# Output-projection products placed in the last head pair of a hybrid decoder step (one Trainium2 core)

## What is computed

```
h    = ada_norm(x)                                   # modulation from c @ w_ada
proj = h @ w_in
y_pool = pool_mixer(proj[:, :1024])                  # 8 tiles of 128 channels
y_rwkv = rwkv7(proj[:, 1024:])                       # 16 heads of 64 channels = 8 head pairs of 128
mix  = concat([y_pool, y_rwkv]) @ w_out              # 2048 x 2048
x    = x + gate * mix
h2   = ada_norm(x);  x = x + gate_m * moe(h2)        # 16 experts, top 2
```

## Time and profile before

| what | value |
|---|---|
| median of 3 runs | 2084.46 us |
| lowest and highest | 2076.31 and 2084.47 us |
| the profiled execution, own time | 2076.4 us |
| its span, first to last instruction | 2074.8 us |
| PE busy | 1912.3 us, 92% of the span |
| DVE, ACT, POOL busy | 593.2, 306.4, 453.4 us |
| mean granted TensorE clock | 0.968 |

### The profile page before, as it was taken

One profiled execution on the slowest core, in us unless ns is written; L12 is line 12 of the kernel. 1 busy time (PEld: TensorE's weight loads), 2 busy tenths in 40 slices (PEclk: granted clock), 3 DMA queues, 4 the chain that ended last, 5 costly groups with the idle time before them and its releaser, 6 DMA issues. The chain is left out here.

```text
span 2074.8 us, 27843 instructions
## 1 busy us (share of the span) xinstructions
PE 1912.3 (92%) x10685; PEld 979.8 (47%) x10685; DVE 593.2 (29%) x1326; ACT 306.4 (15%) x690; POOL 453.4 (22%) x585
## 2 busy tenths in 40 slices
PE   4579999999999986999699999999999999999996
PEld 2137665555555544776343344433444434444333
DVE  2152144445434543012312121222122222222213
ACT  2001122212221222001300011100011000111002
POOL 0020012112211221100003322233222332223333
PEclk9679999999999998999799999999999999999998
DMA  9894365546654652754089999999999999999992
GB/s 307 305 307 113 90 201 167 176 157 191 186 153 166 182 170 61 234 160 143 1 342 414 413 410 397 392 390 404 397 394 393 392 403 391 396 397 390 403 393 84
DMA packets 248447, 573.80 MB, mean 277 GB/s; under 512 B 10691, under 2 KB 114461, under 8 KB 230899
## 3 DMA queue, kind: packets, MB, share of 16 engines
q1 hardware_dynamic: 244574, 563.76, 73.8%
q0 software_dynamic: 3200, 6.20, 1.3%
q10 hardware_dynamic: 631, 3.27, 0.6%
HBM read 567.78 MB, written 5.65 MB: 276 GB/s over the span
## 5 line engine op out<-in xcount | busy, mean ns | idle before, releaser
L1761 PE MATMUL PS<-ring,xt 128*64 128x512 f32 x2048 | 523.9, 600 | 2.0 <-DVE xt L1873 1.4
L1963 POOL TENSOR_TENSOR x<-x,tmp 128x512 f32<-128x512 f32 (+1 forms) x192 | 244.7, 1276 | 721.6 <-DVE tmp L1882 721.6
L1882 DVE TENSOR_TENSOR tmp<-PS,catT 128x512 f32<-128x512 f32 (+1 forms) x192 | 132.2, 689 | 620.8 <-PE PS L1749 616.6
L1761 PEld LDWEIGHTS PS<-ring,xt 128*64 128x64 f32 x2048 | 166.8, 136 | 294.2 <-issue 275.2
L1793 PE MATMUL PS<-ring,att 128*64 128x512 f32 x1024 | 226.7, 592 | 0.0
L698 PE MATMUL PS<-ring 128*128 128x320 f32 x672 | 223.1, 457 | 0.0
L1749 PE MATMUL PS<-catT,pwt 128*128 128x512 f32 (+1 forms) x384 | 209.9, 629 | 4.6 <-DVE tmp L1882 2.7
L1793 PEld LDWEIGHTS PS<-ring,att 128*64 128x64 f32 x1024 | 139.4, 137 | 74.5
L364 PE MATMUL PS<-ring,silT 128*32 128x512 f32 x768 | 107.7, 685 | 41.7 <-DMA ring<-in_w_ada 39.5
L698 PEld LDWEIGHTS PS<-ring 128*128 128x128 f32 x672 | 116.5, 191 | 49.3 <-issue 12.9
L1419 PE MATMUL PS<-catT,ring 128*128 128x320 f32 x512 | 138.5, 432 | 0.0
(11 more groups left out here) (409 smaller groups left out, 1649.8 us busy)
## 6 DMA issues: line engine op xcount, KB each, us to landing
ring<-in_w_gate SPq DMA_DIRECT2D x64, 2048.0 KB, 9.5
ring<-in_w_up SPq DMA_DIRECT2D x64, 2048.0 KB, 13.6
ring<-in_w_down SPq DMA_DIRECT2D x64, 2048.0 KB, 12.1
ring<-in_w_ada SPq DMA_DIRECT2D x48, 2048.0 KB, 9.1
ring<-in_w_in SPq DMA_DIRECT2D x34, 1024.0 KB, 5.8
ring<-in_w_out SPq DMA_DIRECT2D x16, 1024.0 KB, 6.0
x_a<-in_x_prompt ACTq DMA_DIRECT2D x2, 1024.0 KB, 8.2
sraw<-in_state_wkv POOLq DMA_DIRECT2D x8, 256.0 KB, 3.7
```

The source lines that it names most:

```text
L1761: m = nc.tensor.matmul(PS[C * g:C * g + C, c, :], xt[:, 4 * q + k, :], unit(2 * q + g, FE)[:, k, 512 * c:512 * c + 512], start=(q == 0 and ...
L1882: nc.vector.tensor_tensor(tmp[0:n_, r % 2, :], PS[0:n_, 2 + r % 2, :], gtm[0:n_, i // 2, 512 * c:512 * c + 512], ALU.mult).then_inc(sc_ev, 1)
L1963: nc.gpsimd.tensor_tensor(xx, xx, tmp[0:n_, r % 2, :], ALU.add).then_inc(x_ok, 1)
```

## The change

The last pair gets filling products of its own: matmuls of the output projection's first three column tiles, contraction tiles 0 to 14 of 16, taken with the contraction tile outside and the column tile inside. Tile 15 is the last pair's own output and stays in phase_mix, where products (0, 0), (0, 1) and (0, 2) now consist of this one matmul each. Banks 0 to 2 hold the sums across the phase boundary, so the 27 shift transposes go through banks 3 to 6 in two parts, 16 and 11, with a copy after each.

```
-            sp.wait_ge(sh_ev, 1)
+            sp.wait_ge(sh_ev, 2)
...
+            def mixed(j, k, i):
+
+                if k == 0:
+                    pe.wait_ge(G["s_wo"][j], 16)
+                    pe.wait_ge(z_done, i + 1)
+                elif k == KT - 2 and j == 0:
+                    pe.wait_ge(fin, i)
+                nc.tensor.matmul(PS[:, j, 0:T], G["wo"][:, j, k, :], catT[:, k, :], start=(k == 0), stop=False)
...
-                units = iter([] if last else [(j, k) for j in (1, 0, 2) for k in range(KT)])
+                units = iter([(j, k) for k in range(KT - 1) for j in range(3)] if last else
+                             [(j, k) for j in (1, 0, 2) for k in range(KT)])
 
                 def fill(n):
                     for _, (j, k) in zip(range(n), units):
-                        project(j, k, i)
+                        if last:
+                            mixed(j, k, i)
+                        else:
+                            project(j, k, i)
...
             for j in range(27):
-                n = min(P, SH - j * P)
-                m = nc.tensor.transpose(PS[0:NC9, j // 4, (j % 4) * P:(j % 4) * P + n], zlast[0:n, j, :],
+                n, r = min(P, SH - j * P), j % 16
+                if j == 16:
+                    m.then_inc(t_sh, 1)
+                    pe.wait_ge(sh_ev, 1)
+                m = nc.tensor.transpose(PS[0:NC9, 3 + r // 4, (r % 4) * P:(r % 4) * P + n], zlast[0:n, j, :],
                                         ident[0:n, 0:n])
             m.then_inc(t_sh, 1)
...
             act.wait_ge(t_sh, 1)
-            nc.scalar.copy(shrow[:, 0:27 * P], PS[0:NC9, 0:7, :].rearrange("p b n -> p (b n)")[:, 0:27 * P]
+            nc.scalar.copy(shrow[:, 0:16 * P], PS[0:NC9, 3:7, :].rearrange("p b n -> p (b n)")).then_inc(sh_ev, 1)
+            act.wait_ge(t_sh, 2)
+            nc.scalar.copy(shrow[:, 16 * P:27 * P], PS[0:NC9, 3:6, :].rearrange("p b n -> p (b n)")[:, 0:11 * P]
                            ).then_inc(sh_ev, 1)
...
-                for k in range(KT):
+                for k in range(KT - 1 if g == 0 and j < 3 else 0, KT) if isinstance(g, int) else range(KT):
                     m = nc.tensor.matmul(PS[:, j, 0:T], wo[:, j, k, :], catT[:, k, :], start=(k == 0),
                                          stop=(k == KT - 1))
```

## The result

The changed kernel takes 2087.26 us (median of 10 runs, 2085.65 to 2089.68). The kernel before, measured beside it, takes 2076.32 (10 runs, 2074.91 to 2085.26). The ratio is 1.0044, 95% interval 1.0029 to 1.0059 (the medians of the two stand 10.9 us apart, the means 9.1): slower, by a little less than the 0.5% that the prediction took for its bound. The time lies in the range 2083 to 2102, but 8.4 us under the forecast of 2095.7. On the profiled execution's own time the forecast was 2087.6; the profiled execution of the changed kernel took 2087.37.

The account below looks back on a forecast made before the run. PE was taken to bound the mix but not pair 7, where holes stood open. The terms, +24.4 - 14.9 + 1.65 = +11.2 us, on the median of 2084.46 gave 2095.7 us, range 2083 to 2102.

Parts of the forecast that it names:

- the last line of the sum: Whole kernel: the shift of +11.2 us put on the median of the runs shown, 2084.46, giving 2095.7 us.
- The bound of 0.5%: Whole kernel: 10.4 us, about what a measurement can tell from no change; slower got 0.56, same 0.42, faster 0.02.
- The upper bounds: High ends of the terms at the bonus matmul, the mix's wait and handing over; the shift was given as +7 to +15.
- The wait in the first filling: Pair 7: PE stands for three w_out tiles from 762.7 to 785.3, so the bonus matmul starts at 791.8, before 769.64.
- the half clock lasts longer: Rival, pair 7: PE stays at half clock through nine units and the transposes behind; +15.7 us, 2100.2; chance 0.12.
- The shift rows: Tail between pair 7 and the mix: the two-part transposes and copies take 9.3 us instead of 10.59.
- The mix: Product (1,0) waits 9.4 us for its w_out tile; 14.9 us gained instead of 24.2, less 1.65 by the clock.
- The tile overtakes the unit: Rival, mix: the w_out tile lands before the 2 MB unit issued ahead; about +5 us, 2089.5; chance 0.10.
- The weights are in time: Rival, pair 7: the three w_out tiles land by about 763.7, so the kernel is 8.4 us faster, 2076.1; chance 0.03.

Follow-up runs that it names:

- e5: The kernel before, with contraction tiles 0 to 14 of products (0,0), (0,1) and (0,2) of the mix computed nowhere; 2068.22 us.
- e6: The kernel before, with only the shift transposes split in two parts through banks 3 to 6; 2079.71 us.
- e8: The changed kernel, with filling units taken column by column, so the first 11 need one w_out tile instead of three; 2082.94 us.
- e1: The changed kernel, with SP issuing the first three w_out tiles ahead of the last pair's two w_ada reloads; 2068.20 us.
- e2: The changed kernel, with the first 2 MB unit of expert weights issued behind the first three w_out tiles of the mix; 2081.40 us.
- e3: The changed kernel with both load orders changed, that is the edits of e1 and e2 together; 2061.71 us.
- e4: The kernel before, with PE made to wait for the three w_out tiles at the last pair's first filling, and no filling; 2097.64 us.
- e7_fill_only: The kernel before, with 45 matmuls on data already in SBUF filling the last pair, and the mix left whole; 2083.50 us.

## Why the prediction was right in its sum and wrong in its time

**The step that failed** is the last line of the sum: "on the median it is **2095.7 us**, 0.54% more". It put the shift of +11.2 us on the median of three runs, 2084.46. Of the ten runs measured beside the changed kernel three lie at 2084.46 to 2085.26 and seven at 2074.91 to 2076.40; two of those three high ones had been among the first three. The median of ten is 2076.32, within 0.1 us of the profiled execution's own time (2076.4), and 2076.32 + 11.2 = 2087.5, measured 2087.26. The 47 later runs of the kernel before, beside the experiments, have medians of 2076.49 and 2077.39; only four of them reach 2084.4. The reason given, "the shift does not depend on what makes that difference", was true of the shift and says nothing of the base. The prediction saw that the profiled execution was 8.1 us below the median, and that the runs went down to 2076.31, and took the higher without saying why three runs should tell the base. The shift in per cent was off less: +10.9 us by the medians is 0.53%, and the ratio says 0.44%. The bound of 0.5% lies between them, so whether "slower" (0.56) or "the same" (0.42) came true hangs on less than these runs can tell.

**The sum was right in part by luck.** Pair 7 was forecast at +25.7 us and came at +26.0, the tail at -1.3 and came at -0.4, the mix at -13.25 and came at -14.6: two misses of about 1 us each way. And the profile of before has a pair 7 that is 1.8 us shorter than in e5 and e6. The upper bounds add up to +15.6, not +15; nothing hung on that.

**The wait in the first filling: right.** Counted from where pair 7 began (3.15 us earlier than before), the bonus matmul was forecast at 791.8 and came at 792.3, the score products at 795.6 and 795.9, the variance matmul at 843.3 and 843.7, the mix at 852.6 and 853.9. The third tile came 0.7 us sooner than forecast, 781.47 + 3.15 = 784.6. Inside the filling one term was small by 1.2 us: nine units took 7.7 us, not 6.5, since the clock, forecast to be back 3.3 us after the third tile, was still at 0.50 from 782 to 786 and at 0.96 at 787. The scan ran at 1.00, as forecast, and the rival "the half clock lasts longer" was true for 2 us and not for the pair.

**The shift rows: wrong by 0.9 us.** Forecast -1.3, measured -0.4. The 11 transposes behind ACT's first copy were costed at full clock (1.35 us) and took 2.32, at 0.50 in the row of 846 us, after PE had idled 1.94 us. That is the whole miss: in e8 (its last row) they took 1.38 us after an idle time of 1.95, and the tail was 9.30 us there, as in e1 and as forecast. So the split was costed rightly and the clock of these transposes was not. Why it fell in after, e2 and e3 and not in e1 and e8, behind the same idle time, stays open.

**The mix: right in its mechanism, two terms off against each other.** The tile was forecast 22.8 us after the start and came at 20.84; the wait was 6.47 us and not 9.4. The unit ahead of it landed 14.5 us after its issue instead of 16.6, and SP was free of it after 7.05 us instead of 8.95:

```profile
L1343 SPq DMA_DIRECT2D ring<-in_w_gate x1: 7050/7050/7050, 853.4 to 853.4; - x1
DMA to landing us min/median/max: 14.5/14.5/14.5
```

The prediction took the unit's landing from the kernel before, as if the change left it alone. Against that the product behind the wait lost 2.2 us by the clock, not 1.65. Together the mix gained 14.6 us, forecast 13.25.

**The rivals.** *The tile overtakes the unit*: it did not in any run. The unit landed at 853.38 + 14.5 = 867.9, and PE went on at 871.6. That is also how the trace stands to the rule of the Trainium skill, "DMA: Bandwidth & Descriptors", section "Queues, rings and completion order", which says that completion is not first-in, first-out per issuing engine. Its own example is a later transfer that runs on one DMA engine only, and no run here was made to test that. In all ten profiles the tile issued next behind the unit landed after it, by 3.4 to 3.7 us, and what changed the time was the order of issue (e2). *The weights are in time*: it did not happen in this change, but e1 makes its condition true, and its forecast of -8.4 us stands against -8.3 there by the medians (2068.20 against 2076.49 beside it). By the stages it is -10.6 us (108.51 against 119.06), so the close agreement is luck as well: pair 7 took 5.4 us more and not 6.2, and the mix gave 14.6 and not 13.25. This was the mechanism that decided the sign, and its point (the tiles landed by about 763.7) was the right thing to ask for.

## What to carry to other kernels

Before work is moved into a hole, ask when its operands land, and read that from the queue that issues them: here a hole of 7 us was offered to matmuls the last of whose weights came 22 us after the hole began, and the order of a few lines on SP was worth 20.65 us where the matmuls themselves were worth 24.2. Work that is taken out of a stretch also covers the loads behind it; cost the next wait before the gain is booked. And take the base of a forecast from the same execution as the durations, or, where the runs shown differ by as much as the effect, say on which of them it stands.

## What was not expected of the hardware

The granted clock came back only 5.5 to 6 us after continuous matmuls began again (0.50 from 782 to 786, 0.96 in 787 to 788, start 781.47), where the same pair of the kernel before had shown some 3.5 us. Without the filling (e4) it rose only some 11 us after the wait ended at 780.12 (0.69 in 790 to 792, 1.00 in 792 to 794), and was at 0.50 once more from 796 to 804, while the pair's own small matmuls ran. So a wait can cost more than the delay at its place (20.8 us for 15.2 in e4), and how much depends on what follows it.

The 2 MB unit at the start of the mix landed 16.6 us after its issue in the three kernels whose pair 7 is neither filled nor held up, and 14.5 to 15.4 us in the five where it is one or both, though the loads issued around it are the same. No run tells why; it was worth 2 to 3 us of the second wait.

The first head pair starts at 264.73 to 276.23 us in the ten profiles, 11.5 us apart in executions that do the same work up to there. The waits for `w_ada` do not account for it: PE waited 39.5 us for it before the pairs in before, and 37.8 in e7_fill_only, where they began 8 us later. The larger part of these 8 us, 5.5, is the clock. The 48 transposes of `x` near the beginning took 9.2 to 9.7 us in eight of the profiles, at a granted clock of 1.00 in before, and 14.7 us in the two that began the pairs latest, e1_loads_first and e7_fill_only, at 0.50 all through with PE busy without a break. First before, then e7_fill_only:

```profile
42.92 9.24 PE L286 MATMUL PS<-ident,x_a 128*128 128x128 f32 x48
```

```profile
45.37 14.74 PE L286 MATMUL PS<-ident,x_a 128*128 128x128 f32 x48
```

What kept the clock down through 14.7 us of unbroken work stays open, and so does the rest of the scatter. Whether the three runs of the kernel before near 2085 us are such executions cannot be told; only profiled executions show their phases.
